# Hybrid RG-LRU and attention layer: attention's DVE steps recorded one item later, gate tiles in three parts, sinks and decay constants set up during the first norm

## The reference, cut to what matters

```
z = h @ w_in + b_in                      # split into xr, gr, q, k, v, ga, mg
hr = rg_lru(causal_depthwise_conv(xr))   # block gates, a scan over positions
y_a = (hr * silu(gr)) @ w_rnn_out
q, k = rope(q), rope(k)
o = sliding_window_sink_attention(q, k, v, sinks)
y_b = (o * silu(ga)) @ w_attn_out
mixed = sigmoid(mg_A) * y_a + sigmoid(mg_B) * y_b
out = layer_norm(alpha * h + mixed @ w_o + b_o)
```

## Time and profile before

| what | before |
|---|---|
| median of 3 runs | 2665.57 us (2581.42 to 2734.97) |
| the profiled execution | 2580.33 us |
| its span on the slowest core (core 1) | 2578.8 us |
| spans of the 8 cores | 2568.4 to 2578.8 us |
| mean granted clock of the 8 cores | 0.969 to 0.972 |
| PE busy | 2360.1 us (92%) |
| DVE busy | 1294.3 us (50%) |
| ACT busy | 899.9 us (35%) |
| POOL busy | 170.6 us (7%) |

### The profile page before, as it was taken

How to read it: one execution, slowest core, us unless ns; L and a number is a source line. 1 busy time by engine, 2 the same in 40 slices (tenths; PEclk the granted TensorE clock), 3 DMA queues, 4 the chain that set the end, 5 groups by cost and what they waited for, 6 DMA issues and landing times.

```text
span 2578.8 us, 33027 instructions; the slowest of 8 cores (2568.4 to 2578.8 us)
## 1 busy us (share of the span) xinstructions
PE 2360.1 (92%) x11560; PEld 1073.1 (42%) x11560; DVE 1294.3 (50%) x1686; ACT 899.9 (35%) x1517; POOL 170.6 (7%) x314
## 2 busy tenths in 40 slices
PE   1789998799989999999998999989999999999996
PEld 1533333344544444444444433333444444444442
DVE  5745555587764446311454545556777542111145
ACT  0215556555661013210330554556555210010033
POOL 0000000001000000011000000000000000100100
PEclk9889999899999999999998999989999999999998
DMA  8243432244438998766954433323443796654563
GB/s 217 53 83 53 75 61 48 41 71 69 69 53 193 224 205 169 130 108 95 243 183 107 81 59 63 65 45 54 74 71 67 174 230 142 118 95 74 87 207 115
DMA packets 93249, 281.77 MB, mean 109 GB/s; under 512 B 29312, under 2 KB 40192, under 8 KB 80272
## 3 DMA queue, kind: packets, MB, share of 16 engines
q0 software_dynamic: 44640, 159.40, 38.6%
q1 hardware_dynamic: 48448, 120.26, 14.2%
HBM read 390.74 MB, written 37.75 MB: 166 GB/s over the span
## 4 chain that ended last, share of the span: by engine, by line
PE 61%; DVE 16%; ACT 9%; issue 6%; DMA 5%; SPq 2%; DVEq 0%; ACTq 0%; POOL 0%; POOLq 0%
PE ps L424 61%; ACT s_all L398 8%; DVE s_all L412 8%; DMA s_all<-w_o 3%; DVE s_all L888 3%; DVE s_all L408 2%; SPq L533 2%; DVE s_all L401 2%; DMA s_all<-be_bc 1%; DVE s_all L415 1%; DVE s_all L475 1%; DMA s_all<-s_all 1%; ACT L381 1%; DMA s_all<-sink_rows 0%; PE ps L489 0%
## 5 line engine op out<-in xcount | busy, mean ns | idle before, releaser
L424 PE MATMUL ps<-s_all 128*128 128x512 bf16 (+6 forms) x11288 | 2343.1, 377 | 134.9 <-ACT s_all L398 55.4
L424 PEld LDWEIGHTS ps<-s_all 128*128 128x128 bf16 (+3 forms) x11288 | 1055.6, 100 | 1416.9 <-issue 343.3
L398 ACT ACTIVATE s_all<-ps,s_all 128x512 f32<-128x512 f32 (+2 forms) x432 | 255.3, 643 | 924.0 <-PE ps L424 778.1
L412 DVE SCALAR_TENSOR_TENSOR s_all<-s_all 128x1040 f32<-128x1040 f32 (+5 forms) x324 | 481.1, 1485 | 149.3 <-ACT s_all L398 111.7
L398 ACT ACTIVATE s_all<-s_all 128x512 f32<-128x512 f32 (+7 forms) x501 | 369.9, 739 | 439.8 <-DVE s_all L412 155.1
L412 DVE SCALAR_TENSOR_TENSOR s_all<-s_all,ps 128x512 f32<-128x512 f32 x128 | 87.5, 686 | 539.4 <-PE ps L424 538.7
L398 ACT ACTIVATE s_all<-ps 128x512 bf16<-128x512 f32 (+4 forms) x409 | 226.5, 622 | 296.0 <-PE ps L424 255.2
L401 DVE TENSOR_TENSOR s_all<-s_all 128x512 bf16<-128x512 f32 (+5 forms) x330 | 189.6, 584 | 229.1 <-ACT s_all L398 200.0
L412 DVE SCALAR_TENSOR_TENSOR s_all<-ps,s_all 128x512 f32<-128x512 f32 (+3 forms) x276 | 187.9, 723 | 86.2 <-DMA s_all<-r_s 45.9
L433 POOL DMA_DIRECT2D s_all<-w_in x196 | 109.4, 559 | 1779.2 <-PE ps L424 1753.4
L726 DVE TENSOR_TENSOR s_all<-s_all 128x1024 bf16<-128x1024 bf16 x124 | 85.4, 689 | 111.1 <-ACT s_all L398 111.1
(11 more groups left out here) (13 smaller groups left out, 102.7 us busy)
## 6 DMA issues: line engine op xcount, KB each, us to landing
s_all<-w_in POOLq DMA_DIRECT2D x196, 512.0 KB, 6.1
s_all<-x SPq DMA_DIRECT2D x32, 1024.0 KB, 8.5
s_all<-w_attn_out POOLq DMA_DIRECT2D x32, 512.0 KB, 6.9
s_all<-w_rnn_out POOLq DMA_DIRECT2D x32, 512.0 KB, 6.9
r_s<-s_all SPq DMA_DIRECT2D x16, 1024.0 KB, 6.2
s_all<-w_o POOLq DMA_DIRECT2D x32, 512.0 KB, 9.8
s_all<-r_s SPq DMA_DIRECT2D x16, 1024.0 KB, 6.6
out<-s_all SPq DMA_DIRECT2D x16, 1024.0 KB, 4.5
```

The costliest lines, as they stand in the source:

```text
L398: P.op("act", lambda e: e.activation(out=out, in_=in_, func=func, **kw), rd, wr)
L412: P.op("dve", lambda e: e.scalar_tensor_tensor(out=out, in0=a, scalar=s, in1=b, op0=op0, op1=op1), rd, [out])
L424: P.op("pe", lambda e: e.matmul(out, lhsT=lhsT, rhs=rhs, start=start, stop=stop), [lhsT, rhs], [out], signal=stop)
```

## The change: what it does

- `item()` runs one attention item and after it the functions that the item before left in `late`. The mask of scores() and the output steps of weighted() are put into `late`, so they are recorded on DVE after the matmuls and ACT functions of the next item. `lt` becomes two buffers in turn.
- A head has 18 items, the last but one empty, at 18/16 and 18/11.5 items a chunk.
- A gate chunk is recorded in three parts: its first DVE step at its own chunk, its ACT functions at the next gate chunk, its products at the one after. `ga_step(None, None, None)` moves the parts on without a new chunk.
- The sinks are loaded once, behind the load of x block 4, and their exps, PM's memsets and the decay constants' ACT functions stand between stage_a(0) and stage_a(1).

```diff
+    lts = [lt, sb("lt1", [512], F32, F0 + 18432)]
...
+        late = [[]]
+
+        def item():
+            ready, late[0] = late[0], []
+            if att_q:
+                att_q.pop(0)()
+            for f in ready:
+                f()
+
+        def drain():
+            while att_q or late[0]:
+                item()
...
             while budget[0] >= 1.0:
                 budget[0] -= 1.0
-                if att_q:
-                    att_q.pop(0)()
+                item()
...
-                memset(PM[0][:], 0.0)
-                memset(PM[1][:], 0.0)
...
             stage_a(0)
+            load("sp", "sk", lt[64:72, :], sink_d)
+            for i in range(2):
+                memset(PM[i][:], 0.0)
+                act(PM[i][64:72, :], lt[64:72, :], AF.Exp)
+            table("natural_log_exp_and_others")
+            act(cl[:], lam, AF.Exp, scale=-1.0)
+            act(cl[:], cl[:], AF.Ln, bias=ONE_T)
             stage_a(1)
+            ts(hcl[:], cl[:], -4.0, None, ALU.mult)
+            ts(cl[:], cl[:], -8.0, None, ALU.mult)
...
             table("natural_log_exp_and_others")
-            for i in range(2):
-                load("sp", f"sk{i}", lt[64:72, :], sink_d)
-                act(PM[i][64:72, :], lt[64:72, :], AF.Exp)
-            act(cl[:], lam, AF.Exp, scale=-1.0)
-            act(cl[:], cl[:], AF.Ln, bias=ONE_T)
-            ts(hcl[:], cl[:], -4.0, None, ALU.mult)
-            ts(cl[:], cl[:], -8.0, None, ALU.mult)
...
-            P.op("dve", lambda e: e.tensor_tensor(out=v, in0=v, in1=m, op=ALU.mult), [pt[:], msk], [pt[:]])
+            late[0].append(lambda: P.op("dve", lambda e: e.tensor_tensor(out=v, in0=v, in1=m, op=ALU.mult), [pt[:], msk], [pt[:]]))
...
+            lt_ = lts[n % 2][:]
...
+            def out():
+                if kh == 0:
+                    tt(dst, v4(ob), v4(lt_), ALU.mult)
+                else:
+                    tt(ogt[:], ob, lt_, ALU.mult)
+                    tt(dst, v4(ogt[:]), dst, ALU.mult)
+            late[0].append(out)
...
-                if n < 8:
-                    items.append(lambda n=n: ev(n))
+                items.append((lambda n=n: ev(n)) if n < 8 else (lambda: None))
                 items.append(lambda n=n: od(n))
...
+        steps = [[], []]
+
+        def ga_step(first, second, third):
+
+            for f in steps[1]:
+                f()
+            steps[1] = []
+            for f, g in steps[0]:
+                f()
+                steps[1].append(g)
+            steps[0] = []
+            if first is not None:
+                first()
+                steps[0].append((second, third))
...
-        rate[0] = 17.0 / 16.0
+                def first(z=z, zb=zb):
+                    ts(z, zb, bin_c[:, TGA + j:TGA + j + 1], -80.0, ALU.add, ALU.max)
+
+                def second(z=z, g=g):
+                    act(g, z, AF.Exp, scale=-1.0)
+                    act(g, g, AF.Ln, bias=ONE_T)
+                    act(g, g, AF.Exp, scale=-1.0)
+
+                def third(z=z, g=g, dst=dst):
+                    if mult:
+                        tt(g, z, g, ALU.mult)
+                        tt(dst, g, dst, ALU.mult)
+                    else:
+                        tt(dst, z, g, ALU.mult)
+                ga_step(first, second, third)
+
+        rate[0] = 18.0 / 16.0
...
             ga_tile(4 * kh + 5, False)
+            ga_step(None, None, None)
...
             ga_tile(4 * kh + 7, False)
-            while att_q:
-                att_q.pop(0)()
+            ga_step(None, None, None)
+            ga_step(None, None, None)
+            drain()
...
-        rate[0] = 17.0 / 11.5
+        rate[0] = 18.0 / 11.5
         budget[0] = 0.0
         load_wg(0)
         ga_tile(0, True)
+        ga_step(None, None, None)
         xr_tile(0)
+        ga_step(None, None, None)
         xr_tile(1)
         conv(0)
         conv(1)
         for j in range(1, 4):
             ga_tile(j, True)
-        while att_q:
-            att_q.pop(0)()
+        ga_step(None, None, None)
+        ga_step(None, None, None)
+        drain()
```

More of the change, by code:

```diff
@@ L752, in weighted @@
                         mm(bank[r0:r0 + 64, :], seqs[half][si][0], seqs[half][si][1], si == 0, si == ns - 1)
-            act(lt[:], db, AF.Ln)
-            act(lt[:], lt[:], AF.Exp, scale=-1.0)
+            lt_ = lts[n % 2][:]
+            act(lt_, db, AF.Ln)
+            act(lt_, lt_, AF.Exp, scale=-1.0)
             q0 = n * 128
@@ L781, in do_pass, with ga_tile @@
         gctr = [0]
-        def ga_tile(j, late):
+        steps = [[], []]
[10 more added lines that the diff above has]
+                steps[0].append((second, third))
+        def ga_tile(j, mult):
             w = wtile(w_in_d[TGA + j])
@@ L790, in ga_tile @@
                 gctr[0] += 1
[L791 to L795, removed]
-                dst = og[:, j, cs - OFF:cs - OFF + n]
[L797 to L801, removed]
-        rate[0] = 17.0 / 16.0
+                z, g = gz[i][:], gs[i][:]
+                dst = og[:, j, cs - OFF:cs - OFF + n]
+                def first(z=z, zb=zb):
[12 more added lines that the diff above has]
+        rate[0] = 18.0 / 16.0
         for kh in range(3):
```

## The result

The changed kernel takes 2507.47 us (median of 4 runs, 2506.45 to 2507.78). The ratio to the kernel before is **0.9716, 95% interval 0.9701 to 0.9731**: 2.8% faster. Some executions of any kernel are disturbed and longer (the four of before spread from 2581.42 to 2930.51 us, with a median of 2700.27), and the ratio leaves these out, so the change is worth some 73 us and not the 193 us between the medians. The mean clock rose from 0.969 to 0.972, to 0.984 to 0.985. The change adds a line ahead of what it moves, so L425 answers to L424 before, L399 to L398, L402 to L401, L409 to L408, L739 (mask) to L726.

What follows compares the result with a forecast made beforehand. The prediction took TensorE, busy 92%, as the bound, with gaps from an ACT and DVE ping-pong in the attention stages. 2580.3 - 35 - 28 + 1.3 = 2518.6, so 2519 us; range 2492 to 2572, its own case 2506 to 2541.

Steps and rivals of the forecast that it cites:

- A: The forecast itself as a case: 2519 us, own range 2506 to 2541, chance 65%.
- term 1: Attention heads 0 to 2, both passes: gaps from the ACT and DVE ping-pong and at head ends go, -35 us.
- term 2: Head 3, both passes, up to the gate stage: shorter despite a wait behind conv, -28 us.
- term 3: The setup: gap behind the norms removed, -12.84 us, but norm 1 waits for sinks and constants, +14.1; net +1.3 us.
- my end of -41: Heads 0 to 2: the far end of term 1, all excess over 76.1 us a head and head 0's end gaps gone.
- The cover of 2 us in q chunks: In q chunks, the 2 us left before TensorE would wait for a mask recorded behind the rope on DVE.
- DVE is the longer: Head 3 of pass 1: DVE's work behind conv, not TensorE's, sets the end; 76 us, -15 us.
- the exchange of 12.84 for 14.1: Setup: moves go out 12.84 us earlier without the sinks behind the norms, while the norms run 14.1 us later.
- the lower end: Setup: sinks ready as soon as the constants (42.0 us), norm 1 only 8.7 us later, net -4 us.
- B: Rival: conv eats head 3, masks and outputs behind it stop TensorE twice, term 2 gives nothing; 2547 us, 17%.
- C: Rival: gaps come from scores' banks or ACT's sum, which recording order leaves; only end gaps go; 2564 us, 12%.
- D: Rival: slower, weighted() waits for the mask behind the rope in 24 q chunks; 2615 us with one whole rope, 6%.

Runs made afterwards that it cites:

- only_late: Kernel before with only the masks and weighted outputs recorded one item late, with two lt buffers; ratio to before 0.9791.
- only_gates: Kernel before with only the gate chunks recorded in three parts; ratio to before 0.975.
- masks_now: Changed kernel with masks and weighted outputs recorded with their own item again, three-part gates and empty item kept; ratio to before 0.9716.
- seventeen: Changed kernel without the empty item, 17 items a head at 17/16 and 17/11.5, held steps ahead of the last item; ratio to before 0.9726.
- flush_conv: Changed kernel with the held masks and outputs recorded in front of conv in head 3; ratio to before 0.9688.
- no_setup: Changed kernel with sinks, PM's memsets and decay constants back at their old places, two sink loads behind the norms; ratio to before 0.9708.
- setup_only: Kernel before with only the setup moved as in the change; ratio to before 0.998.
- early_sinks: Changed kernel with sinks and constants issued before x block 2, PM's memsets at the start, one table load fewer; ratio to before 0.9669.

## Why the prediction was right in its mechanism and off in its size

2519 was forecast and 2507.5 measured, inside the range, and the case was A. The sum was too small: against the profiled execution of before it said -61.7 us (2.4%), and the span of core 1 fell by 73.9 (2.8% by the ratio). **The step that failed is the size of term 1**: -35 was taken and -44 measured. It left 1 us at the end of each of six heads for a late DVE, and nothing was late there; and it took -41 for the most that the heads could give. Of the 12.2 us missing, term 1 has 9.2 and term 2 0.5, and 5.7 lie in stretches that the forecast left at nothing (about what the cores of one kernel differ by in them); term 3 came out 3.2 us worse on core 1.

2519 is also 5.5% under the median shown before the change (2665.57), and 6.7% under that with its fourth run (2700.27): twice what came, and more. As a forecast against these medians it is off; it was made for executions like the profiled one, and these are what the ratio compares.

**What bounds it**: right. The ping-pong of ACT and DVE was the loss, shown by the waits of before and after, and by only_late and only_gates, which each remove it and each give most of the gain.

**Term 1, -35 forecast, -44 measured.** The failed step, in its words: "I leave 1 us for each of six heads". Nothing was late at the ends of heads, TensorE runs through them. That is 6 us. The other 3 go past my end of -41: heads of 75.2 us, below the 76.1 that the pair of the earlier trace rows gives for eight. Two places per head now have two items in a row, one before; that this saves a switch between projections and items is argued only. The forecast "76 to 78 us apart" was too high; gaps gone and clock 1.00 were right. The cover of 2 us in q chunks held: no wait for L739 in 240.28 us. What I did not see is that the three edits overlap: gates in three parts and either of the others would have done nearly as well (masks_now, seventeen).

**Term 2, -28 forecast, -28.5 measured.** The schedule held in detail for pass 0: conv at T+38 (430.03, with T = 392.28), forecast T+38; the mask behind it done at T+50.1 (442.35), forecast T+50.5; the wait 5.28 us, forecast about 7; head 3 at 78.6, forecast 78. In pass 1 the wait was 3.35 and head 3 took 79.8, forecast 76. The levels of the forecast end earlier, at the group of 16 matmuls that starts at 501.04 and 1757.20 before, 2.1 us ahead of the table load; the group's weight loads begin at 468.73 and 1684.45 now, so by the forecast's own marker head 3 took 76.5 us in pass 0 (1.5 under) and 76.7 in pass 1 (0.7 over).

For pass 1 the reason given was wrong all the same. "DVE is the longer" added 22.70 + 3 + 1 us of DVE behind a conv that ends at T+45.5. conv ended at T+47.4 (1655.15, with T = 1607.77), and from TensorE's return to the table load TensorE was nearly full and DVE was not (columns as above):

```profile
1655.90:1687.57 31.67, 29.96 (x143) 11.65 (x144) 20.20 (x31) 21.18 (x36) 1.05 (x2) 0.89 0.23 39
```

DVE had 20 us of work there, not 26.7; what was left for TensorE, part of it at half clock, set the end. That the level came within 1 us is luck.

**Term 3, +1.3 forecast, +4.5 on core 1, +2.4 in the mean of four cores.** The square root ran from 49.89 to 50.18 (forecast: ends at 49.6), and the last table load behind the norms 15.6 us later (forecast 14.1): the exchange of 12.84 for 14.1 had the right mechanism and sign. The rest is in the chain of moves: from the table load to the first scores 15.6 - 4.5 = 11.1 us came back, not 12.84; SP was still issuing moves when they started. What of these 1.7 us is a cost and what is chance of the kind told in the last section, is open. The memsets (1.02 us for both, at 31.70) lay in the wait, as said. On the table load the trace decides: from the start of a load to the next function are 46.66 to 47.96 us and 48.59 to 49.89, 1.30 each, and the square root came where the earlier trace rows puts it. The Trainium skill (ScalarE: Activation LUTs, What ACT_TABLE_LOAD costs) has 2.66 us for it, by which the square root would have come 2.8 us later; the trace disagrees. On the order of landing, the sinks came with block 4 (ACT used them 13.4 us after their issue; the block landed in 13.5 us, 13.4 before), not before it: the lower end did not come about.

**Rivals.** B: the wait behind conv is there, but single, and the gain of head 3 is 28.5 us, not 0. flush_conv shows what it costs: 4.6 us in pass 0; in pass 1 recording order in front of conv saves next to nothing (0.4 us). C: refuted; the ends of heads are a part only, 9 us a head went. D: refuted; ropes and held masks share DVE without one wait on TensorE.

**Open:** whether the 2 to 4 us that the setup move costs at the first scores reach the end (the intervals of no_setup and the changed kernel overlap; in the mean spans of cores 0 to 3, over the executions that the ratios use, no_setup is 2.2 us below the changed kernel, 2499.0 and 2501.2, but setup_only is 2.1 below before, 2571.4 and 2573.5); why a head takes 75.2 us rather than 76.1; what sets the last landing of the moves.

## What to carry to other kernels

When two engines that run in order feed each other, look for the instruction that stands waiting ahead of the one the other engine needs, and record it one unit of work later; a single break in the chain can give most of it (61 and 51 of 77 us here, though the third gives 21), so try the parts one by one before keeping all (here masks held late add nothing to gates in three parts and an empty item, and cost a wait behind conv). Before a long step on such an engine, release what you hold. A small load that an in-order engine will wait for belongs early on its queue, with as few large ones in front of it as can be: here that was worth some 12 us, as much as the gap of 11.68 us that the move was to fill.

## What the runs showed of the hardware

Equal gaps cost different amounts. In front of the first scores, at the same place of the same code, TensorE was idle for 3.12 us on core 1 of the changed kernel and for 3.10 us on core 3 of masks_now. The windows of 4 us behind the two gaps (columns as before), the changed kernel's first:

```profile
168.83:172.83 4.00, 4.00 (x10) 1.25 (x11) 2.01 (x3) 1.55 (x3) 0.00 (x0) 0.50 0.09 25
```
```profile
169.05:173.05 4.00, 4.00 (x19) 1.78 (x20) 2.01 (x3) 1.55 (x3) 0.00 (x0) 1.00 0.09 25
```

10 matmuls at 1.2 GHz against 19 at 2.4. It goes both ways at other lengths too: behind 2.66 us on core 1 of setup_only the clock stayed at 1.00, behind 2.68 us on core 2 of early_sinks it was 0.50. It costs 2 to 3 us each time (setup_only was 4.1 us late at the first scores and only 1.3 at the end of head 0), so a difference of that size between single stretches of two kernels proves nothing about an edit. What decides it, these runs don't show.

A load of 16 KB right behind one of 1024 KB on the same queue was there only when the large one was, in both places where it stood. Behind x block 4 it was issued at 32.10 us and used at 45.50, 13.4 later (the block: 13.5). In early_sinks it stands in front of the x blocks 2 and 3 but right behind be_bc, 1024 KB with 26.1 us from issue at 2.91 to landing: issued at 3.38, it was used at 29.81, 26.4 later. What the move gained is the earlier issue; the way stayed long.
